# Weight slots of a float32 transformer kernel: high and low parts woven in one slot, and low parts of wide products on multiples of 256 bytes

## The reference

```python
def hybrid_layer(x, ...):             # first block, one layer
    h = rms_norm(x, norm_g) * (1.0 + scale) + shift
    ... = jnp.split(h @ w_in, IN_OFFSETS, axis=-1)      # four attention branches
    term = jax.nn.sigmoid(h @ w_merge[i]) * (yi @ w_br[i])   # four times, summed
    ...                               # times w_out, added to x

def second_block(x, mem, ...):        # two layers
    # layer 0: conformer convolution; layer 1: differential attention with shared k, v
    x = x + memory_cross_attention(rms_norm_2(x, norm_mem[i]), mem, w_q, w_k, w_v, w_o)
    x = x + swiglu(rms_norm_2(x, norm_ffn[i]), w_gate, w_up, w_down)   # hidden width 2816
    ...

def swiglu(h, w_gate, w_up, w_down):
    return (jax.nn.silu(h @ w_gate) * (h @ w_up)) @ w_down
```

## Time and profile before

| what | value |
|---|---|
| median of 3 runs (lowest to highest) | 1111.04 us (1110.3 to 1111.07) |
| profiled execution, span from first to last instruction | 1111.3 us |
| PE busy | 1092.0 us, 98% |
| PEld busy | 951.6 us, 86% |
| DVE busy | 749.5 us, 67% |
| ACT busy | 583.6 us, 53% |
| DMA, mean | 176 GB/s |
| mean granted TensorE clock | 0.997 of full speed |

### The profile page before, as it was taken

How to read it: one execution, slowest core, us unless ns; L and a number is a source line. 1 busy time by engine, 2 the same in 40 slices (tenths; PEclk the granted TensorE clock), 3 DMA queues, 4 the chain that set the end, 5 groups by cost and what they waited for, 6 DMA issues and landing times.

```text
span 1111.3 us, 15418 instructions
## 1 busy us (share of the span) xinstructions
PE 1092.0 (98%) x6251; PEld 951.6 (86%) x6251; DVE 749.5 (67%) x1024; ACT 583.6 (53%) x940; POOL 54.4 (5%) x87
## 2 busy tenths in 40 slices
PE   8999999999999999999999999999999999999997
PEld 6799988788898988989988988788988989888986
DVE  5736776865679977555678855546967546788643
ACT  3458653444477775555444544456765545444442
POOL 3311000000010000001000000000011000000000
PEclk9999999999999999999999999999999999999999
DMA  9956464655654325535555555544445435555550
GB/s 343 381 161 207 135 196 162 233 184 189 223 168 126 115 77 189 175 99 149 197 184 184 196 182 196 189 153 151 152 153 189 132 115 190 190 190 189 162 179 38
DMA packets 118776, 195.09 MB, mean 176 GB/s; under 512 B 6586, under 2 KB 39762, under 8 KB 118705
## 3 DMA queue, kind: packets, MB, share of 16 engines
q1 hardware_dynamic: 116144, 187.51, 50.7%
q0 software_dynamic: 2560, 6.60, 2.0%
HBM read 193.04 MB, written 1.05 MB: 175 GB/s over the span
## 4 chain that ended last, share of the span: by engine, by line
PE 83%; DVE 10%; ACT 5%; issue 1%; DMA 1%; POOL 1%; SPq 0%; DVEq 0%; ACTq 0%; POOLq 0%
PE product L669 55%; PE small L706 5%; PE product L706 5%; DVE conv_out L2719 5%; PE product L708 3%; PE small L708 3%; PE product L996 3%; ACT w_high L591 1%; ACT diagonal L2612 1%; DVE w_low L601 1%; PE small L816 1%; PE small L2081 1%; PE small L731 1%; PE small L1462 1%; PE small L1451 1%
## 5 line engine op out<-in xcount | busy, mean ns | idle before, releaser
L601 DVE TENSOR_TENSOR w_low<-w_raw,w_high 128x2048 fp32r<-128x2048 f32 (+3 forms) x160 | 350.0, 2190 | 180.2 <-ACT w_high L591 178.6
L591 ACT ACTIVATE w_high<-w_raw 128x2048 fp32r<-128x2048 f32 (+3 forms) x160 | 292.1, 1832 | 175.9 <-PE product L669 144.2
L669 PE MATMUL product<-w_high,H 128*128 128x512 f32 (+2 forms) x736 | 239.7, 393 | 0.5 <-DVE w_low L601 0.5
L669 PEld LDWEIGHTS product<-w_high,H 128*128 128x128 f32 x736 | 137.9, 188 | 26.9 <-DVE w_low L601 0.9
L669 PE MATMUL product<-H,w_high 128*128 128x256 f32 x816 | 150.9, 283 | 0.1
L669 PE MATMUL product<-w_low,H 128*128 128x512 f32 (+2 forms) x368 | 142.3, 387 | 0.0
L669 PEld LDWEIGHTS product<-H,w_high 128*128 128x128 f32 x816 | 126.6, 188 | 1.1 <-DVE w_low L601 0.5
L669 PE MATMUL product<-H,w_low 128*128 128x256 f32 x408 | 114.2, 280 | 0.0
L706 PE MATMUL product<-H,w_high 128*128 128x512 f32 x256 | 89.1, 391 | 0.0
L706 PE MATMUL small<-H,w_high 128*128 128x512 f32 x256 | 89.1, 391 | 0.0
L669 PEld LDWEIGHTS product<-w_low,H 128*128 128x128 f32 x368 | 69.3, 188 | 11.9 <-issue 0.2
(11 more groups left out here) (412 smaller groups left out, 1784.3 us busy)
## 6 DMA issues: line engine op xcount, KB each, us to landing
w_raw<-in_ffn_w_gate SPq DMA_DIRECT2D x20, 1024.0 KB, 5.0
w_raw<-in_ffn_w_up SPq DMA_DIRECT2D x20, 1024.0 KB, 5.0
w_raw<-in_ffn_w_down SPq DMA_DIRECT2D x20, 1024.0 KB, 5.0
w_raw<-in_w_merge SPq DMA_DIRECT2D x16, 1024.0 KB, 5.2
w_raw<-in_w_ada SPq DMA_DIRECT2D x32, 256.0 KB, 6.5
w_raw<-in_mem_w_k SPq DMA_DIRECT2D x8, 1024.0 KB, 5.0
w_raw<-in_mem_w_v SPq DMA_DIRECT2D x8, 1024.0 KB, 5.0
w_raw<-in_conv_w_pw SPq DMA_DIRECT2D x16, 512.0 KB, 4.7
```

Source lines behind the costliest of these rows:

```text
L591: k.act.eng.activation(parts_of(k, i, j)[0], raw_of(k, i), ACT.Copy).then_inc(*k.act.tells("weights_high", ("weights high", i)))
L601: k.vec.eng.tensor_tensor(low, raw, high.bitcast(F32), ALU.subtract).then_inc(*k.vec.tells("weights_low", ("weights low", i)))
L669: mm = pe.eng.matmul(bank[:, off:off + wide], a, r, start=b not in started, stop=True, skip_group_check=True)
```

## The change

The high and the low slots are merged into three slots of 16384 bytes and 8 words, each 224 bytes past a multiple of 256 (`SLOT`, `SLOT_AT`).
- `still` chunks are woven: element 0 of high, element 0 of low, element 1 of high and so on. High begins at a multiple of 256, low 4 bytes later, and the elements of either part are 8 bytes apart. ScalarE writes, VectorE reads and writes, and TensorE's loads read with that step.
- `apart` chunks keep high at remainder 224, with low now at a multiple of 256.
- `turned` chunks have both parts at multiples of 256, as before; high and low are now 8192 bytes apart.
- The room for statistics at the end grows from 432 to 600 words. The arrays behind it begin 96 bytes lower, those between the slots and it 768 bytes lower; the operand pairs behind it are aligned to 256 again.

No instruction is added, removed or moved: each engine has the same operations in the same order in both kernels, and only addresses, and in `still` chunks the step between elements, are other ones.

```diff
-HIGH_ROOM, LOW_ROOM = 8, 16
-HIGH_AT = {"turned": 8, "still": 0, "apart": 0}
-LOW_AT = {"turned": 16, "still": 8, "apart": 4}
+SLOT, SLOT_AT = 2 * CK * CN + 8, 56
+HIGH_AT = {"turned": 8, "still": 8, "apart": 0}
+LOW_AT = {"turned": 8 + CK * CN, "apart": 8 + CK * CN}
...
-        self.w_high, self.w_low, self.w_first, self.rooms, self.used, self.st = [], [], [], [], [], {}
-        for slots, name, more in ((self.w_high, "w_high", HIGH_ROOM), (self.w_low, "w_low", LOW_ROOM)):
-            for i in range(self.N_SPLIT):
-                self.room(LINE // 4 - more)
-                if slots is self.w_high:
-                    self.w_first.append(self.sb(f"w_first{i}", [P, CK * CN], at=self.at))
-                slots.append(self.sb(f"{name}{i}", [P, CK * CN + more], F32R))
+        self.w_slots, self.w_first, self.rooms, self.used, self.st = [], [], [], [], {}
+        for i in range(self.N_SPLIT):
+            self.room(SLOT_AT)
+            self.w_first.append(self.sb(f"w_first{i}", [P, CK * CN], at=self.at))
+            self.w_slots.append(self.sb(f"w_slot{i}", [P, SLOT], F32R))
...
-        self.room(432)
+        self.room(600)
...
 def parts_of(k, i, j):
 
-    kind = k.plan[i][2][0]
-    return [chunk_view(k, t[j][:, at[kind]:], i) for t, at in ((k.w_high, HIGH_AT), (k.w_low, LOW_AT))]
+    kind, slot = k.plan[i][2][0], k.w_slots[j]
+    if kind == "still":
+        both = slot[:, HIGH_AT[kind]:HIGH_AT[kind] + 2 * CK * CN].rearrange("p (n two) -> p n two", two=2)
+        return [chunk_view(k, both[:, :, part], i) for part in range(2)]
+    return [chunk_view(k, slot[:, at[kind]:], i) for at in (HIGH_AT, LOW_AT)]
```

## The result

| kernel | median (lowest to highest) | runs |
|---|---|---|
| before | 1111.05 us (1110.04 to 1113.57) | 6 |
| after | 1116.31 us (1114.83 to 1117.66) | 5 |

The ratio is 1.0041, with a 95% interval of 1.0027 to 1.0055: the change makes the kernel slower by 5 us (3.0 to 6.1 by the interval), where 8 us faster was forecast. One more run of the kernel after, 1564.64 us at a granted clock of 0.654 in place of 0.998, is left out.

What follows compares the result with a forecast made beforehand. PE, busy 98% of the span, was taken as the bound. Still matmuls 5.3 + 1.8 us and apart pairs 1.3 us gave 8.4 us less than the median of 1111.04: 1102.6 us, range 1095 to 1118.

Steps and rivals of the forecast that it cites:

- L2973 is no transpose, as ours, so I take 111.3 ns: 5.5 ns less: Still matmuls: new distance taken from unsplit matmuls of 128 columns, 111.3 ns against 116.75; 5.3 us plus 1.8 us less.
- the pace of the load: Float32r stream at twice the load's pace makes the excess, 10.1 ns on a still matmul; weaving takes most away.
- bounded the distance by 106.7 and 126.9: Still matmuls: 106.7 ns if only the columns count, 126.9 if the load's doubled reach doubled the excess.
- unsplit float32 rows: Transposes at 110 ns and unsplit matmuls of 128 columns at 111.3, read as load and stream of equal pace.
- woven loads hinder the stream more: Rival for still matmuls: excess goes with places a load touches; doubled excess, 10 ns each, 1126 us, chance 0.17.
- mild form: Same rival, smaller: 3.3 ns more on 960 + 324 still matmuls, 2.9 us more in all, 1114 us; chance 0.12.
- 1284 of the 1608 matmuls: Still matmuls passing on their change: 960 where PE is busy throughout, and half of the other 648, 324.
- The 1.3 us for low at 0: Apart pairs: low weights go from remainder 208 to 0, 2.6 ns less on each of 512 pairs.
- With 227.1 + 116.75: Apart pairs: a turned and a still matmul's times summed to 343.9 ns a pair in place of 346.5.
- 0.1 us from small copies: ACT's split with an 8-byte step: 5 ns for 128 elements, 0.1 us for 2048, on 1.91 us; counted as 0.

Runs made afterwards that it cites:

- e4_loads_step2: The kernel before, where only TensorE's still loads read with a step of 8 bytes and the splits stay plain: 1116.16 us in one run.
- e8_one_column_loads: The kernel before, with each still load reading one column of weights 128 times (step 0): 1107.93 us in one run.
- e6_half_streams: The kernel before, with still matmuls from the second tile on moving 128 columns instead of 256: 1103.45 us in one run.
- e1_plain_line: The kernel before, with both parts of still chunks plain and begun at remainder 0 in place of 224: 1114.49 us, ratio 1.0028.
- e3_slots_only: The kernel after without weaving: merged slots, low apart parts at 0, still parts plain and both at remainder 224: 1114.2 us, ratio 1.0032.
- e9_x_224: The kernel before, with x (`H`) begun at remainder 224 in place of 0, `mem` and weights keeping their remainders: 1118.93 us, ratio 1.0075.
- e12_still_64: The kernel after without weaving, plain still parts begun 64 bytes past a multiple of 256: 1106.22 us, ratio 0.996 to before.
- e11_after_plain: The kernel after with only the weaving undone, still parts plain and both at remainder 0: 1113.5 us, ratio 1.0027.
- e10_plain_192: The kernel before, with plain still parts begun at remainder 192 in place of 224: 1111.81 us, ratio 1.001.
- e5_x_adjacent: The kernel before, with x's high and low rows side by side, so a pair's 512-column stream is one run: 1110.67 us, ratio 1.0004.

## Why the prediction was wrong

**The failed step** is "L2973 is no transpose, as ours, so I take 111.3 ns: 5.5 ns less", with the reading under it that the pace of the load makes the excess and weaving takes it away. Still matmuls measured 3.3 ns more, not 5.5 less. The pace is refuted by `e4_loads_step2`: an 8-byte step alone makes the distance longer (+4 ns at 224). A load that doesn't move at all still leaves 113.3 to 120 ns (`e8_one_column_loads`). I had called the cause inferred, and bounded the distance by 106.7 and 126.9, which holds 120; but I took the middle from unsplit float32 rows (110 and 111.3 ns), and these can't tell a load's own time from a stream's excess. `e6_half_streams` shows nearly the same, 111.1 ns, for float32r with half the stream, where the load is the longer side. So those rows fit the time of a load by itself, and gave nothing on a stream of 256 columns beside one.

**What I left out** is the remainder. I noted that still parts go from 224 to 0 and priced only the step, so the address stood at nothing in the sum, without a reason. `e1_plain_line`, with no other change, loses 3.6 us by it (1114.49 against 1110.86), against 5.3 us in the kernel after. `e3_slots_only` has the old distance again, and `e9_x_224` shows that it is a distance to the stream and not an alignment in itself. The rival that won is "woven loads hinder the stream more" in its mild form: its 3.3 ns were the ones measured, and its 1114 us are 2.3 us short of the result. That the number fits is luck. The result lies in my range only because I drew it that far for this rival. Its cause, the reach over twice the bytes, may hold at 224, where weaving costs 4 ns; in the kernel after it is not the cause, since plain parts at 0 take as long.

**What is hidden.** I let 1284 of the 1608 matmuls count, 80%. It was a little less: in `e1_plain_line` 3.6 us arrive of 1608 x 3.2 = 5.1, 70%, and in `e12_still_64` 4.4 of 6.2, as much. By this share the kernel after should lose 3.6 to 4.2 us by its still matmuls. Its medians say 5.3 and its profiled span 4.5, but the interval of 3.0 to 6.1 us holds all of these.

**Apart pairs.** The 1.3 us for low at 0 did not come: 346.6 ns for a pair, as before. The step "With 227.1 + 116.75" took the address as the cause. The same addresses give 353.3, 346.6 and 344.5 ns, by what runs ahead of them. A gain of 1.1 us was there with plain parts at 0 or 64 (`e11_after_plain`, `e12_still_64`). With low at 208 the pairs took 346.7 ns whatever the still chunks did (`e1_plain_line`, `e4_loads_step2`, `e8_one_column_loads`, `e10_plain_192`).

**The splits** were right where it matters: DVE unchanged, ACT hidden. ACT's step of 8 bytes costs some 180 ns a split, about 10%, where I had read 0.1 us from small copies; twelve of 64 by 128 elements against two of 128 by 128 were a thin base for that the earlier trace rows.

**The base.** The profiled execution of before was not 0.3 us above the median but about 1.5 us: its span is 1111.3 us, while the ordinary runs have spans of 1108.8 to 1109.8 us and times 1.3 us above them. The forecast itself went by the median and stays at 1102.6 us; against the span it would have been 1102.9 us of span, which is some 1104.2 us of time. Differences of profiled spans are less sure than those of medians: instruction by instruction, the profiled execution of before is 2.3 us behind that of `e5_x_adjacent`, 0.8 by 58 us and 1.4 between 178 and 231 us, with pairs and still matmuls alike.

**The two rules.** In the Trainium skill, TensorE: Matmul & The Clock Gate, step 1 of Part 2, says that the load has a read port of its own and takes nothing from the running matmul. The runs disagree: the same stream takes 113.5, 116.8 or 120 ns for 256 columns by where the load reads. In the Trainium skill, SBUF — State Buffer, the note on cachelines under Door 1, a step of two float32 has two hits on a line of 16 bytes and so is free. The runs agree for DVE's split (2290 ns both) and disagree for ACT's (1911 to 1952 in the mean) and for a load at 224 (+4 ns).

**Still open.** Between `e11_after_plain` and the kernel after stand 2.8 us. In the long runs still matmuls differ by 0.1 ns, pairs by 2.1 ns x 512 = 1.1 us. Of the rest the two traces place a part: their spans are 2.5 us apart, and the kernel after is 0.7 us behind at the start of its first run of 96 (226.34 against 225.63 us), ahead of any pair. The runs of one kernel spread over 2 to 3 us. Why a distance of 64 is good, by what memory what ran before acts, and whether 64 would stay good with other chunks around it was not tried further.

## What to carry over

The distance between TensorE's weight load and its stream, by 256 bytes, is a parameter to be scanned and then confirmed in a whole kernel, since neither "aligned" nor one chunk's value tells what it gives. Change the address and the layout in separate kernels: here the merged slots gave pairs at 353.3, 346.6 or 344.5 ns by how the still chunks lay, so the parts of the edit can't be priced one by one and added. When a price is taken from rows of another operation, ask first which side limits those rows.

## What the hardware showed that was not expected

- The pace of float32r matmuls of 256 columns depends on the load's start against the stream's: 120.0 ns with both at the same remainder by 256 (0 and 0, or 224 and 224), 116.7 at 224 against 0, 113.5 in most chunks at 64 against 0.
- In turned matmuls of `H`, 512 columns, it is the other way about: some 227 ns with both at 0, 229 to 237 with the weights elsewhere, 232.4 with `H` at 224.
- Something is carried over from what ran before: 256 pairs at unchanged addresses took 353.3 or 344.5 ns each by the address of the four still chunks ahead, and 344.4 and 353.3 in the two layers of one kernel. Inside one chunk the distance of still matmuls went from some 118 to 113.3 ns at a break.
- A load with a step of 8 bytes adds 4 ns at 224 and nothing at 0.
- A load of 128 columns beside a stream of 128 takes 111 ns: halving the stream from 256 columns gained only 5.7 of 116.8 ns.
